# The product of decay matrix and inputs in fp32r parts in a state-space block

## The reference

```python
xf = (x.astype(jnp.float32) * dt[..., None]).reshape(bsz, nc, ln, g, hg, p)
seg = a_cum[:, :, :, None] - a_cum[:, :, None]
decay = jnp.exp(jnp.where(causal, seg, -jnp.inf))
cb = jnp.einsum('bclgn,bcsgn->bclsg', cc, bc)
y_diag = jnp.einsum('bclsgh,bcsghp->bclghp', cb[..., None] * decay, xf)
```

## Time and profile before

| | us |
|---|---|
| median of 3 runs | 2071.91 |
| profiled execution | 2075.03 |
| its span | 2073.0 |
| TensorE busy | 2059.2 (99%) |
| VectorE busy | 1199.0 (58%) |
| ScalarE busy | 1012.7 (49%) |
| GpSimd busy | 189.0 (9%) |

### The profile page before, as it was taken

One profiled execution on the slowest core, in us unless ns is written; L12 is line 12 of the kernel. 1 busy time (PEld: TensorE's weight loads), 2 busy tenths in 40 slices (PEclk: granted clock), 3 DMA queues, 4 the chain that ended last, 5 costly groups with the idle time before them and its releaser, 6 DMA issues.

```text
span 2073.0 us, 28214 instructions
## 1 busy us (share of the span) xinstructions
PE 2059.2 (99%) x9508; PEld 1711.8 (83%) x9508; DVE 1199.0 (58%) x1329; ACT 1012.7 (49%) x1238; POOL 189.0 (9%) x210
## 2 busy tenths in 40 slices
PE   8999999999999999999999999999999999999999
PEld 7888888888888888888888888888888888888887
DVE  4665566656666667666655555555545544554554
ACT  5545555555555454545554444444334434444443
POOL 2110010000012111111210000001001000000000
PEclk9999999999999999999999999999999999999999
DMA  7565555665566665666565656566666666666665
GB/s 227 169 175 170 169 163 172 182 182 172 174 203 183 190 195 184 195 199 191 173 183 184 193 187 231 181 188 187 193 193 183 190 195 185 188 190 192 185 189 163
DMA packets 197437, 385.97 MB, mean 186 GB/s; under 512 B 11985, under 2 KB 12945, under 8 KB 197089
## 3 DMA queue, kind: packets, MB, share of 16 engines
q1 hardware_dynamic: 195920, 381.15, 60.8%
q10 hardware_dynamic: 960, 2.75, 0.4%
q0 software_dynamic: 464, 0.77, 0.1%
HBM read 382.46 MB, written 2.16 MB: 186 GB/s over the span
## 4 chain that ended last, share of the span: by engine, by line
PE 98%; DVE 1%; DMA 1%; ACT 0%; issue 0%; POOL 0%; DVEq 0%; POOLq 0%; ACTq 0%
PE ps L462 31%; PE ps L464 31%; PE ps L463 30%; PE ps L430 3%; PE ps L687 1%; DMA raw<-in_w_in 1%; PE ps L516 0%; PE ps L539 0%; PE ps L676 0%; PE ps L697 0%; DVE wlo L1254 0%; DVE cacc L1447 0%; ACT whi L841 0%; PE ps L540 0%; PE ps L517 0%
## 5 line engine op out<-in xcount | busy, mean ns | idle before, releaser
L1254 DVE TENSOR_TENSOR wlo<-raw,whi 128x1024 fp32r<-128x1024 f32 x703 | 893.5, 1276 | 690.0 <-ACT whi L841 685.9
L841 ACT ACTIVATE whi<-raw 128x1024 fp32r<-128x1024 f32 x703 | 740.6, 1060 | 704.3 <-PE ps L464 690.0
L462 PE MATMUL ps<-whi,xT_hi 128*128 128x512 f32 x1276 | 511.0, 400 | 4.6 <-DVE xT_lo L1275 4.6
L464 PE MATMUL ps<-whi,xT_lo 128*128 128x512 f32 x1276 | 499.4, 391 | 0.0
L463 PE MATMUL ps<-wlo,xT_hi 128*128 128x512 f32 x1276 | 498.3, 390 | 0.0
L462 PEld LDWEIGHTS ps<-whi,xT_hi 128*128 128x128 f32 x1276 | 240.6, 189 | 52.6 <-DVE xT_lo L1275 5.1
L464 PEld LDWEIGHTS ps<-whi,xT_lo 128*128 128x128 f32 x1276 | 240.1, 188 | 51.3
L463 PEld LDWEIGHTS ps<-wlo,xT_hi 128*128 128x128 f32 x1276 | 240.7, 189 | 47.9 <-issue 1.0
L462 PE MATMUL ps<-whi,hT_hi 128*128 128x512 f32 x512 | 200.8, 392 | 1.0 <-issue 1.0
L462 PE MATMUL ps<-whi,fT_hi 128*128 128x512 f32 x512 | 199.7, 390 | 0.0
L464 PE MATMUL ps<-whi,hT_lo 128*128 128x512 f32 x512 | 199.6, 390 | 0.0
(11 more groups left out here) (253 smaller groups left out, 1839.8 us busy)
## 6 DMA issues: line engine op xcount, KB each, us to landing
raw<-in_w_in SPq DMA_DIRECT2D x319, 512.0 KB, 3.8
raw<-in_w_up SPq DMA_DIRECT2D x128, 512.0 KB, 4.0
raw<-in_w_down SPq DMA_DIRECT2D x128, 512.0 KB, 4.2
raw<-in_w_ssm_out SPq DMA_DIRECT2D x64, 512.0 KB, 4.3
raw<-in_w_attn_out SPq DMA_DIRECT2D x32, 512.0 KB, 4.3
raw<-in_w_out SPq DMA_DIRECT2D x32, 512.0 KB, 4.3
arow<-arows SPq DMA_DIRECT2D x16, 512.0 KB, 5.0
h<-in_x ACTq DMA_DIRECT2D x1, 2048.0 KB, 10.5
```

What stands on the lines that cost most here:

```text
L462: mm(dst, xh, whi[sl][:, kk, :], start=(s == 0 and kk == 0), stop=False)
L464: last = mm(dst, xl, whi[sl][:, kk, :], start=False, stop=(s == US - 1 and kk == UK - 1))
L841: A(whi[s % SLOTS][:, :, :], raw[s % SLOTS][:, :, :], ACT.Copy).then_inc(hi_ready, 1)
L1254: V.tensor_tensor(wlo[s % SLOTS][:, :, :], raw[s % SLOTS][:, :, :], fp(whi[s % SLOTS][:, :, :]), ALU.subtract).then_inc(lo_ready, 1)
```

## The change

The product is done in fp32r parts. M is rounded (`M_hi`, ScalarE) and its remainder kept (`M_lo`, VectorE). xf is likewise split into a rounded part (ScalarE) and a remainder (GpSimd), which lie side by side in `xf_hl`. For each head the rounded matrix meets both parts in one matmul with 128 columns, and the remainder of the matrix meets the rounded part in one with 64 columns, accumulating into the first 64 of those. The result takes two banks (4 and 5), and VectorE adds it in two steps.

M_hi lies where arow was, so SP's load of arow now waits for the product of the block before instead of for the differences, and it is placed ahead of unit 3 of the block instead of ahead of unit 0. In ScalarE's order exp moves from step 2 to step 1; in VectorE's M moves from step 3 to step 2.

```diff
@@ sync
-            def load_block(b, w, row0, col0):
+            def load_block(b, w, row0, col0, rows=None):
                 for s in range(SLOTS if isinstance(b, int) and b == 0 else 0, US):
+                    if rows and s == 3:
+                        rows()
                     sp.wait_ge(lo_ready, US * b + s - SLOTS + 1)
...
                 if later(n):
-                    sp.wait_ge(seg_raw, n)
+                    sp.wait_ge(y_mm, n)
...
@@ tensor
             def ssd_y(n, c, g):
                 def f():
-                    pe.wait_ge(M_ready, n + 1)
-                    pe.wait_ge(xf_ready, n + 1)
+                    pe.wait_ge(M_hi_ready, n + 1)
+                    pe.wait_ge(M_lo_ready, n + 1)
+                    pe.wait_ge(xf_lo_ready, n + 1)
                     if c == 0:
                         pe.wait_ge(cb01_ready, g + 1)
                     for hh in range(HG):
-                        last = mm(ps[6][:, hh * SHD:(hh + 1) * SHD], M[:, hh, :], xf[:, hh, :], start=True,
-                                  stop=True)
+                        dst = ps[4 + hh // 4]
+                        o = hh % 4 * P
+                        mm(dst[:, o:o + P], M_hi[:, hh, :], xf_hl[:, hh, :, :].rearrange("p a d -> p (a d)"),
+                           start=True, stop=False)
+                        last = mm(dst[:, o:o + SHD], M_lo[:, hh, :], xf_hl[:, hh, 0, :], start=False, stop=True)
@@ scalar
+            def xf_round(n):
+                def f():
+                    act.wait_ge(xf_ready, n + 1)
+                    A(xf_hl[:, :, 0, :], xf[:, :, :], ACT.Copy).then_inc(xf_hi_ready, 1)
+                return f
+
+            def M_round(n):
+                def f():
+                    act.wait_ge(M_ready, n + 1)
+                    A(M_hi[:, :, :], M[:, :, :], ACT.Copy).then_inc(M_hi_ready, 1)
+                return f
...
-                    steps(b, {2: [ssd_exp(n)], 7: [z_sigmoid(b, g)]})
+                    steps(b, {0: [xf_round(n)], 1: [ssd_exp(n)], 3: [M_round(n)], 7: [z_sigmoid(b, g)]})
                 else:
                     steps(b, {1: [conv_first(11)], 3: [conv_silu(11, cT[:, :, :])], 4: [conv_out(11)],
-                              6: [ssd_exp(n)], 7: [z_sigmoid(b, g)]})
-                steps(b + 1, {2: [ssd_exp(n + 1)], 6: [y_squares(g)], 7: [agate(b + 1, j)]})
+                              5: [xf_round(n), ssd_exp(n)], 6: [M_round(n)], 7: [z_sigmoid(b, g)]})
+                steps(b + 1, {0: [xf_round(n + 1)], 1: [ssd_exp(n + 1)], 3: [M_round(n + 1)], 6: [y_squares(g)], 7: [agate(b + 1, j)]})
...
@@ vector
+            def ssd_M_lo(n):
+                def f():
+                    dve.wait_ge(M_hi_ready, n + 1)
+                    V.tensor_tensor(M_lo[:, :, :], M[:, :, :], fp(M_hi[:, :, :]), ALU.subtract).then_inc(M_lo_ready, 1)
+                return f
+
             def ssd_y(n, c, g):
                 def f():
                     dve.wait_ge(y_mm, n + 1)
                     dve.wait_ge(skip_ready, n + 1)
-                    V.tensor_tensor(xs_at(g, c), xs_at(g, c), ps[6][:, :], ALU.add).then_inc(yd_done, 1)
+                    parts = ps45[:, :, :].rearrange("p b (h a d) -> p (b h) a d", a=2, d=SHD)
+                    xh = heads(xs_at(g, c), HG)
+                    V.tensor_tensor(xh, xh, parts[:, :, 0, :], ALU.add).then_inc(yh_done, 1)
+                    dve.wait_ge(yh_done, n + 1)
+                    V.tensor_tensor(xh, xh, parts[:, :, 1, :], ALU.add).then_inc(yd_done, 1)
...
-                    steps(b, {0: [ssd_seg(n, 0, g)], 1: [ssd_cbm(n, 0, g)], 3: [ssd_M(n)], 5: [ssd_y(n, 0, g)], 7: [z_gate(g)]})
+                    steps(b, {0: [ssd_seg(n, 0, g)], 1: [ssd_cbm(n, 0, g)], 2: [ssd_M(n)], 3: [ssd_M_lo(n)], 5: [ssd_y(n, 0, g)],
+                              7: [z_gate(g)]})
...
-                              6: [ssd_cbm(n, 0, g)], 7: [ssd_M(n), z_gate(g), ssd_y(n, 0, g)]})
+                              6: [ssd_cbm(n, 0, g), ssd_M(n)],
+                              7: [ssd_M_lo(n), z_gate(g), ssd_y(n, 0, g)]})
...
@@ gpsimd
+            def xf_rest(n):
+                pool.wait_ge(xf_hi_ready, n + 1)
+                G.tensor_tensor(xf_hl[:, :, 1, :], xf[:, :, :], fp(xf_hl[:, :, 0, :]), ALU.subtract) \
+                    .then_inc(xf_lo_ready, 1)
...
                 ssd(4 * j, 0, 2 * j)
                 if later(j):
                     y_rstd(2 * j - 1)
+                xf_rest(4 * j)
                 ssd(4 * j + 1, 1, 2 * j)
+                xf_rest(4 * j + 1)
```

More of the change, by code:

```diff
@@ L132, in build @@
         zs = sb("zs", "W", 4 * KB, [P, NTOK, COLS])
+        M_lo = sb("M_lo", "W", 0, [P, HG, P], f32r)
+        M_hi = sb("M_hi", "W", 8 * KB, [P, HG, P], f32r)
         xf = sb("xf", "W", 12 * KB, [P, HG, SHD])
+        xf_hl = sb("xf_hl", "D", 16 * KB, [P, HG, 2, SHD], f32r)
         xd = sb("xd", "W", 14 * KB, [P, HG, SHD])
@@ L195, in build @@
         X_BANK = [6, 7, 4, 5, 2, 3, 6, 7]
-        ps = [ctx.enter_context(nc.psum_tensor(f"ps{i}", [P, 512], f32)) for i in range(8)]
+        ps = [ctx.enter_context(nc.psum_tensor(f"ps{i}", [P, 512], f32)) for i in range(4)]
+        ps45 = ctx.enter_context(nc.psum_tensor("ps45", [P, 2, 512], f32))
+        ps += [ps45[:, i, :] for i in range(2)]
+        ps += [ctx.enter_context(nc.psum_tensor(f"ps{i}", [P, 512], f32)) for i in range(6, 8)]
         SETS = [(ps[0], ps[1]), (ps[2], ps[3]), (ps[4], ps[5])]
@@ L273, in build @@
         xf_ready = sem("xf_ready")
+        xf_hi_ready = sem("xf_hi_ready")
+        xf_lo_ready = sem("xf_lo_ready")
         skip_ready = sem("skip_ready")
@@ L280, in build @@
         M_ready = sem("M_ready")
+        M_hi_ready = sem("M_hi_ready")
+        M_lo_ready = sem("M_lo_ready")
+        yh_done = sem("yh_done")
         cb01_ready = sem("cb01_ready")
@@ L388, in ssd_loads @@
             def ssd_loads(j1):
[L389 to L396, removed]
+                if not isinstance(j1, int):
+                    rows0 = lambda: load_rows(4 * j1 - 4, 2 * j1 - 2, 0)
+                else:
+                    load_rows(0, 0, 0)
+                    rows0 = None
+                load_block(B_SSD + 4 * j1 - 4, w_in, 0, Z0 + 2 * j1 * COLS - 2 * COLS, rows0)
+                load_block(B_SSD + 4 * j1 - 3, w_in, 0, GATE0 + j1 * COLS - COLS,
+                           lambda: load_rows(4 * j1 - 3, 2 * j1 - 2, 1))
+                load_block(B_SSD + 4 * j1 - 2, w_in, 0, Z0 + 2 * j1 * COLS - COLS,
+                           lambda: load_rows(4 * j1 - 2, 2 * j1 - 1, 0))
+                load_block(B_SSD + 4 * j1 - 1, w_attn_out, 0, j1 * COLS - COLS,
+                           lambda: load_rows(4 * j1 - 1, 2 * j1 - 1, 1))
             ssd_loads(1)
@@ L1112, in ssd_blocks @@
                 if later(j):
-                    steps(b, {2: [ssd_exp(n)], 7: [z_sigmoid(b, g)]})
+                    steps(b, {0: [xf_round(n)], 1: [ssd_exp(n)], 3: [M_round(n)], 7: [z_sigmoid(b, g)]})
                 else:
                     steps(b, {1: [conv_first(11)], 3: [conv_silu(11, cT[:, :, :])], 4: [conv_out(11)],
-                              6: [ssd_exp(n)], 7: [z_sigmoid(b, g)]})
-                steps(b + 1, {2: [ssd_exp(n + 1)], 6: [y_squares(g)], 7: [agate(b + 1, j)]})
-                steps(b + 2, {2: [ssd_exp(n + 2)], 7: [z_sigmoid(b + 2, g + 1)]})
-                steps(b + 3, {2: [ssd_exp(n + 3)], 6: [y_squares(g + 1)]})
+                              5: [xf_round(n), ssd_exp(n)], 6: [M_round(n)], 7: [z_sigmoid(b, g)]})
+                steps(b + 1, {0: [xf_round(n + 1)], 1: [ssd_exp(n + 1)], 3: [M_round(n + 1)], 6: [y_squares(g)], 7: [agate(b + 1, j)]})
+                steps(b + 2, {0: [xf_round(n + 2)], 1: [ssd_exp(n + 2)], 3: [M_round(n + 2)], 7: [z_sigmoid(b + 2, g + 1)]})
+                steps(b + 3, {0: [xf_round(n + 3)], 1: [ssd_exp(n + 3)], 3: [M_round(n + 3)], 6: [y_squares(g + 1)]})
             ssd_blocks(0)
@@ L1566, in ssd_blocks @@
                               2: [conv_taps(11, 1, 0), conv_taps(11, 1, 1)],
-                              6: [ssd_cbm(n, 0, g)], 7: [ssd_M(n), z_gate(g), ssd_y(n, 0, g)]})
-                steps(b + 1, {0: [ssd_seg(n + 1, 1, g)], 1: [ssd_cbm(n + 1, 1, g)], 3: [ssd_M(n + 1)], 5: [ssd_y(n + 1, 1, g)],
+                              6: [ssd_cbm(n, 0, g), ssd_M(n)],
+                              7: [ssd_M_lo(n), z_gate(g), ssd_y(n, 0, g)]})
+                steps(b + 1, {0: [ssd_seg(n + 1, 1, g)], 1: [ssd_cbm(n + 1, 1, g)], 2: [ssd_M(n + 1)], 3: [ssd_M_lo(n + 1)],
+                              5: [ssd_y(n + 1, 1, g)],
                               6: [y_gated(g, 0)], 7: [y_norm(g)]})
-                steps(b + 2, {0: [ssd_seg(n + 2, 0, g + 1)], 1: [ssd_cbm(n + 2, 0, g + 1)], 3: [ssd_M(n + 2)], 5: [ssd_y(n + 2, 0, g + 1)],
+                steps(b + 2, {0: [ssd_seg(n + 2, 0, g + 1)], 1: [ssd_cbm(n + 2, 0, g + 1)], 2: [ssd_M(n + 2)], 3: [ssd_M_lo(n + 2)],
+                              5: [ssd_y(n + 2, 0, g + 1)],
```

(7 more changed lines are left out.)

## The result

The changed kernel takes 2107.87 us (median of 4 runs, 2098.63 to 2110.94) against 2072.13 us before (2071.79 to 2072.97): a ratio of 1.0163, 95% interval 1.0144 to 1.0181. It is 36 us slower, where +15.8 us was forecast and 2105 was the upper end of the range. Its profiled execution has a span of 2109.2 us, 36.2 more than before.

What follows compares the result with a forecast made beforehand. TensorE, busy 99% of the span, was taken as the bound. Stalls of 16.8 us less 1.0 for the wide matmul gave +15.8, so 2071.91 + 15.8 = 2087.7 us; own range 2080 to 2099, with rivals 2075 to 2105.

Steps and rivals of the forecast that it cites:

- The sum of the stalls: TensorE waiting for M's remainder, all blocks: 3.0 + 2.3 + 4 x 1.4 + 3 x 1.5 + 7 x 0.2 = 16.8 us.
- n = 0: First block of the state-space stage: TensorE stalls 3.0 us more than before, between 2.0 and 3.5.
- n = 1: Second block: rows of decays load late and delay unit 3's weights; stall 2.3 us, between 0.5 and 3.3.
- Odd blocks: Blocks n = 3 to 15: one more f32 product covers the chain; stall 0.2 us each, 0 without contention.
- the first part's: What bounds the kernel: TensorE, at granted clock 1.00; every microsecond of its stalls goes into the end time.
- Contention: VectorE's differences beside GpSimd's subtract of xf's remainder: 0.6 us longer, between 0 and 0.9.
- The pairs of load and matmul: Product on TensorE: 16 pairs at 108 ns, bounded below by weight loads; change taken as 0, up to +3.0 us.
- Rival (a): Product on TensorE: narrow fp32r matmul takes four passes a column, 2.77 us instead of 1.73; 2104 us; chance 0.15.
- (c): Product on TensorE gets cheaper through quicker narrow fp32r loads, 0.86 us, -13.9 in all; 2073.8 us; chance 0.10.
- The 1.0 us for the wide matmul behind an f32 product: First wide matmul after the product: 0.29 falls to 0.23 us if operand kind is the reason; -1.0 us in all.
- SP's later load: Load of the rows of decays after the previous product: a wait at n = 1 only, covered in later blocks.
- Rival (b): Chain ahead of the product is hidden, no even block stalls, n = 0 and 1 remain; 2074 us; chance 0.13.

Runs made afterwards that it cites:

- dose4: Kernel before, f32 product, with 4 idle reductions on VectorE ahead of M for n >= 1: 2086.52 us, ratio 1.0062.
- dose6: Kernel before, f32 product, with 6 idle reductions on VectorE ahead of M for n >= 1: 2117.26 us, ratio 1.0209.
- fp32r_dose6: Kernel before with the fp32r product form alone (remainders left out) and 6 idle reductions on VectorE: 2126.85 us, ratio 1.0261.
- small_rest: Changed kernel, but from n = 1 GpSimd computes only 1 of 64 columns of xf's remainder: 2087.75 us, ratio 1.0084.
- early_seg: Changed kernel, same work reordered: next block's differences in VectorE's step 6, exp, M and remainder earlier, VectorE's stage unrolled: 2071.93 us, ratio 0.9994.

## Why the prediction was wrong

The chain, its position in the queues and the places of the stalls were right, and so was the size of their sum. What was wrong is the clock, and two smaller terms. Each in turn:

- The sum of the stalls: forecast 16.8 us more, measured 18.1. n = 0: 3.0 forecast, 3.68 - 1.01 = 2.7. n = 1: 2.3, measured 2.60 (ScalarE waited 10.5 us for weights that landed behind the rows). n = 6: 1.4, measured 1.32. n = 8: 1.5, measured 1.90. Odd blocks: 0.2, measured 0.31 to 0.38. Two blocks that follow a drop stalled less, since TensorE itself was late: n = 2 0.87, n = 3 nothing. The forecast's stalls count 0.16 us of restart each; with the restarts (15 x 0.16 - 0.27) the measured sum is about 20.2, 3.4 more than forecast.
- The step that failed is the first part's: at a granted clock of 1.00 "every microsecond of a TensorE stall goes into the end time", and no more. I took the clock of the stage as given, a term of nothing. Five drops added 17.1 us, nearly as much as the stalls, and without them the time would have been inside the range. dose4 and dose6 show that stalls alone bring drops, without the change's form; fp32r_dose6 indicates that the form adds to it. The rows at hand held a hint only: the one stall of 1.01 us had left no drop.
- Contention was mis-sized: 0.6 us, at most 0.9, from one GpSimd operation of 1.04 us. At n = 6 the differences took 1.1 us more. Without the contention the stall there was 0.56 instead of 1.32 us (small_rest). They began 8.6 us ahead of TensorE's turn instead of the 8.2 reckoned, which hid part of the miss.
- The rows held a better reading of the contention. In the earlier trace rows GpSimd ends at 745.95 + 1.04 = 746.99 and VectorE at 746.27 + 1.81 = 748.08, 1.09 later. At n = 6 after, GpSimd ends at 774.70 and the differences at 775.78, 1.08 later; the other 11 blocks with this overlap show 1.07 to 1.09. So an operation of 1.22 us ends about when it would had it begun as GpSimd ended, and the price is what GpSimd still had to run (0.72 us in the earlier trace rows, 1.24 here) less some 0.13.
- In n = 4, 8, 12, where no contention was reckoned, the subtract fell on the normalization: 1.91 us for its two operations instead of 0.88. At n = 8 the stall is 1.21 us in small_rest and 1.90 here, so contention cost 0.7, and the rest of the sum was 0.3 too high.

```profile
716.26 1.91 DVE L1587 TENSOR_SCALAR xs<-xs,grs 128x512 f32<-128x512 f32 x2 [0.92 <-POOL grs L1865]
```

- The pairs of load and matmul: 108 ns forecast for both widths, measured 140 and 80, together 110 ns a pair. Rival (a), four passes, is out, and so is (c). The bound from the loads holds on average. The Trainium skill ("TensorE: Matmul & The Clock Gate", Back-to-back issue gap) gives about 81 ns for a pair of load and matmul with 128 moving columns; the trace does not bear it out, with 140 ns.
- The 1.0 us for the wide matmul behind an f32 product did not come back: it takes 0.31 us behind the fp32r product too, so the kind of operand is not the reason. The product's term is 16 x 0.04 = +0.6 us instead of -1.0.
- SP's later load: hidden from n = 2, as forecast. Rival (b) was wrong as the kernel stood, but early_seg makes it true.

## What to carry to other kernels

Where TensorE is the bound and never idle, price a new wait at its length and then ask for the clock: here every stall of 2.2 us or more cost another 1.7 or 3.4 us, and of those of 1.0 to 2.0 us a good third did. Before adding an operation to a chain between in-order queues, place the whole chain against the consumer's turn, and look for idle steps of the block before; the same work placed there was free in this kernel. A control that delays the old code by as much tells the stall from the new code.

## What the runs showed that I had not expected

A short stall of TensorE was often followed by 3.4 or 6.8 us at half clock, which began between 0.5 us before the engine went on and 2.3 us after. Counted over the stage's stalls, behind its first transposes, in the profiles of all runs: 19 of 19 stalls of 2.2 us or more, 13 of 25 of 1.36 to 2.0, 12 of 41 of 1.0 to 1.32, none of 40 below. Of those 12 six are of fp32r_dose6 and three of dose6. The wait of 1.65 to 1.69 us ahead of the transposes left none in any of the 13 profiles. So the length of a stall does not settle it; what else does stays open. With the same idle reductions the stage spent 37.5 us at half clock with f32 matmuls of 64 columns and 58.0 us with fp32r ones of 128 and 64 columns. Why the form matters behind a stall and not without one stays open.

Where a VectorE operation of 1024 elements with two SBUF operands began while GpSimd worked, it ended 1.07 to 1.09 us after GpSimd's operation did, in 27 places of the stage before and after the change.

An fp32r matmul of 128 moving columns took 140 ns and one of 64 took 80 ns when they alternate, each with its own weight load.
